# A two-block transformer kernel: the first stage's first block by lower and upper rows, an own place for odd heads' logits, and another order at the mixers' ends

## What is computed

```python
mod = (c_act @ w_ada[l] + b_ada[l]).reshape(B, N_MOD, D_MODEL)
h = modulate(rms_norm(x, norm_gain[l, 0]), mod[:, 0], mod[:, 1])
x = x + 0.5 * mod[:, 2][:, None, :] * swiglu(h, ffn_w_gate[l, 0], ffn_w_up[l, 0], ffn_w_down[l, 0])
h = modulate(rms_norm(x, norm_gain[l, 1]), mod[:, 3], mod[:, 4])
x = x + mod[:, 5][:, None, :] * hybrid_mixer(h, ...)
...
def swiglu(h, w_gate, w_up, w_down):
    return (jax.nn.silu(h @ w_gate) * (h @ w_up)) @ w_down
```

## Time and profile before

| | us |
|---|---|
| median of 3 runs (2724.70 to 2727.91) | 2726.28 |
| the profiled execution, its time | 2726.13 |
| its span | 2724.3 |
| PE busy with matmuls / DVE busy / ACT busy | 2656.0 / 1981.2 / 1299.1 |
| 1730 to 1800 (heads of a "b" mixer), 70 us: PE / DVE / ACT busy | 62.34 / 48.72 / 41.49 |
| a raw load from issue to landing: by source, medians | 4.9 to 7.2 |
| the slowest raw load on the chain that ended last (issued at 153.82) | 14.03 |

### The profile page before, as it was taken

The page is one execution under the profiler, slowest core; times in us unless marked ns, Lnnn a source line. Parts: engine busy times, 40 slices in busy tenths (PEclk is TensorE's granted clock), DMA queues, the critical chain, the costliest instruction groups (busy, mean ns, idle before and its releaser), DMA issues.

```text
span 2724.3 us, 34156 instructions
## 1 busy us (share of the span) xinstructions
PE 2656.0 (97%) x13951; PEld 2219.1 (81%) x13951; DVE 1981.2 (73%) x2243; ACT 1299.1 (48%) x1451; POOL 0.8 (0%) x6
## 2 busy tenths in 40 slices
PE   6999999999999999999999999899999999998998
PEld 3888877888888877788888899778888889987887
DVE  4767887877768878877877767677787786856754
ACT  2444565544434566544544534554454454445443
POOL 0000000000000000000000000000000000000000
PEclk8999999999999999999999999999999999999999
DMA  7876864677687864677777758437768767763752
GB/s 278 290 287 218 301 211 166 228 261 253 243 290 249 295 225 157 209 260 260 239 261 243 259 197 287 160 126 275 263 212 284 248 242 245 241 205 112 239 201 92
DMA packets 324595, 634.21 MB, mean 233 GB/s; under 512 B 12370, under 2 KB 92434, under 8 KB 324440
## 3 DMA queue, kind: packets, MB, share of 16 engines
q1 hardware_dynamic: 311904, 620.78, 66.4%
q10 hardware_dynamic: 12536, 11.25, 1.5%
HBM read 630.88 MB, written 8.97 MB: 235 GB/s over the span
## 4 chain that ended last, share of the span: by engine, by line
PE 86%; DVE 9%; ACT 2%; issue 1%; DMA 1%; ACTq 0%; DVEq 0%; SPq 0%
PE bank L1465 19%; PE bank L1467 19%; PE bank L1466 19%; PE acc L1465 8%; PE acc L1467 8%; PE acc L1466 7%; DVE w_both L970 3%; PE bank L1574 1%; PE bank L1526 1%; DVE softmax L1179 1%; PE bank L1719 1%; DVE x L1033 1%; PE acc L1702 1%; DVE w_extra L970 1%; DVE work L1031 1%
## 5 line engine op out<-in xcount | busy, mean ns | idle before, releaser
L970 DVE TENSOR_TENSOR w_both<-raw,w_both 128x2048 fp32r<-128x2048 f32 x412 | 941.4, 2289 | 492.2 <-ACT w_both L549 491.3
L549 ACT ACTIVATE w_both<-raw 128x2048 fp32r<-128x2048 f32 x412 | 786.2, 1912 | 525.5 <-PE bank L1467 326.1
L1465 PE MATMUL bank<-w_both,h 128*128 128x512 f32 (+1 forms) x2016 | 773.7, 384 | 2.1 <-DVE w_both L970 1.8
L1467 PE MATMUL bank<-w_both,h 128*128 128x512 f32 (+1 forms) x2016 | 759.3, 377 | 0.0
L1466 PE MATMUL bank<-w_both,h 128*128 128x512 f32 (+1 forms) x2016 | 758.5, 376 | 0.0
L1465 PEld LDWEIGHTS bank<-w_both,h 128*128 128x128 f32 x2016 | 380.3, 189 | 75.1 <-issue 4.4
L1467 PEld LDWEIGHTS bank<-w_both,h 128*128 128x128 f32 x2016 | 379.9, 188 | 70.8
L1466 PEld LDWEIGHTS bank<-w_both,h 128*128 128x128 f32 x2016 | 380.5, 189 | 66.4 <-issue 1.0
L1004 DVE SCALAR_TENSOR_TENSOR ada_sum<-raw,c_act,ada_sum 128x512 f32<-128x512 f32 x476 | 357.5, 751 | 14.1
L1465 PE MATMUL acc<-w_both,y 128*128 128x512 f32 x896 | 356.4, 398 | 0.9 <-DVE softmax L1179 0.9
L1467 PE MATMUL acc<-w_both,y 128*128 128x512 f32 x896 | 349.5, 390 | 0.0
(11 more groups left out here) (196 smaller groups left out, 2355.3 us busy)
## 6 DMA issues: line engine op xcount, KB each, us to landing
raw<-in_w_ada_all SPq DMA_DIRECT2D x136, 1024.0 KB, 5.3
raw<-in_w_in SPq DMA_DIRECT2D x128, 1024.0 KB, 5.6
raw<-in_ffn_gate_all SPq DMA_DIRECT2D x88, 1024.0 KB, 5.2
raw<-in_ffn_up_all SPq DMA_DIRECT2D x88, 1024.0 KB, 5.4
raw<-in_ffn_down_all SPq DMA_DIRECT2D x88, 1024.0 KB, 5.0
raw<-in_w_branch SPq DMA_DIRECT2D x12, 1024.0 KB, 7.2
raw<-in_w_out SPq DMA_DIRECT2D x8, 1024.0 KB, 5.1
raw<-in_w_conv_out SPq DMA_DIRECT2D x8, 1024.0 KB, 4.9
```

What stands on the lines that cost most here:

```text
L549: activate(halves_of[n][0], src, ACT.Copy).then_inc(high_ready.sem, 1)
L970: tensor(halves_of[n][1], raw_of("unit", s, k, 0)[0], halves_of[n][0].bitcast(F32), ALU.subtract).then_inc(low_ready.sem, 1)
L1465: mm(dst, a_h, b_h, start=start, stop=False, skip_group_check=True)
L1467: return mm(dst, a_l, b_h, start=False, stop=True, skip_group_check=True)
```

## The change

Six edits.

1. *Columns at the start.* The order of loads becomes: lower shift columns (0 to 511), lower scale columns (1024 to 1535), x, two units, then the upper shift and scale columns; each block in two loads of 1 MB. All four bias rows are multiplied first. Block 0 is summed by DVE, block 1 half by PE and half by DVE, block 2 by DVE, block 3 half and half. The sums lie in `acc` instead of the four banks.
2. *First block by rows.* In stage 0 units 1 and 2 change places, so that gate and up have first the units of the lower 512 rows. `first_block` does the lower rows of gate and up for both token tiles (48 matmuls), then the upper modulation, then the upper rows. Only then are the products formed.
3. *Odd heads.* In mixer "b" the logits of odd heads lie in `ada_sum` and `logits_odd` instead of `temp`; `logits(m)` waits for the turn of head m-2 instead of m-1 (in "a" it waited for that of m-2 before, too).
4. *Start of the heads.* The split of one unit moves behind the first normalized head (both mixers).
5. *Row parts between the heads* in "b": one half part now comes after the last turn.
6. *Ends of the mixers.* In "a" ACT copies the third output unit first; in both, DVE splits h, the unit, h in this order. `early` is gone: unit 0 is copied by ACT at the end, and split by DVE only after the first updates of x; unit 1 is copied and split after the first normalized rows.

```diff
+        logits_odd = nc.alloc_sbuf_tensor_at("logits_odd", [P, 768], F32, offset=y_at + (4 * 2 * S + 1152) * 4)
...
-            wide = {"a": P, "b": 3 * P}[kind]
-            first = 576 * (m % 2) if kind == "a" else 0
-            return temp[:, first:first + wide], temp[:, first + wide:first + 3 * wide]
+            if kind == "b":
+                return (ada_sum[:, 0:384], logits_odd[:, :]) if m % 2 else (temp[:, 0:384], temp[:, 384:1152])
+            first = 576 * (m % 2)
+            return temp[:, first:first + P], temp[:, first + P:first + 3 * P]
...
+                k = {1: 2, 2: 1}.get(k, k)
...
-            for p in range(3):
-                sp.dma_start(first_w[:, p], ada_cols[0][:, :, 512 * p:512 * p + 512]).then_inc(first_landed[p].sem, 16)
+            def first_load(q):
+                for part in range(2):
+                    c0 = FIRST_AT[q]
+                    sp.dma_start(first_w[:, q, 4 * part:4 * part + 4],
+                                 ada_cols[0][:, 4 * part:4 * part + 4, c0:c0 + 512]
+                                 ).then_inc(first_landed[q][part].sem, 16)
+
+            first_load(0)
+            first_load(1)
             sp.dma_start(x[:, :, :], t["x"].rearrange("b (t p) n -> p (b t) n", p=P)).then_inc(x_landed.sem, 16)
-            sp.dma_start(first_w[:, 3, 0:4], ada_cols[0][:, 0:4, 1536:2048]).then_inc(first_landed[3].sem, 16)
             load(0)
-            sp.dma_start(first_w[:, 3, 4:8], ada_cols[0][:, 4:8, 1536:2048]).then_inc(first_landed[4].sem, 16)
+            load(1)
+            first_load(2)
+            first_load(3)
             for m, (what, s, k, part) in enumerate(items):
-                if m:
+                if m >= 2:
...
             def end_of_mixer(s, first_out):
 
+                high(s, first_out + 2)
                 for half in range(2):
                     high_of_h(s, 0, half, 4)
-                high(s, first_out + 2)
                 high(s, first_out + 3)
                 for half in range(2):
                     high_of_h(s, 1, half, 4)
-                early(s)
+                high(s + 1, 0)
...
+                mixer = STAGES[s - 1] != "f"
                 update(s - 1, 0, 0)
                 update(s - 1, 0, 1)
+                if mixer:
+                    low(s, 0)
                 norm(s, 0)
                 first = 2 if s == 12 or STAGES[s] == "f" else 1
                 if s < 12:
+                    if mixer:
+                        low(s, 1)
...
-                    if m >= ago:
-                        dve.wait_ge(turned_done.sem, turned_done.at(s, TURNS[kind] * (m - ago + 1)))
+                    if m >= 2:
+                        dve.wait_ge(turned_done.sem, turned_done.at(s, TURNS[kind] * (m - 1)))
...
                 def begin_heads():
                     logits(0)
+                    if kind == "a":
+                        return
+                    normalize(0)
+                    low(s, gates_from + 3)
...
+                        if kind == "a" and i == 1:
+                            low(s, gates_from + 3)
...
+                        if kind == "b" and 0 < i < count:
...
-                for half in range(2):
-                    low_of_h(s, 0, half, 4)
+                low_of_h(s, 0, 0, 4)
+                low(s, WO_A + 2)
+                low_of_h(s, 0, 1, 4)
                 for half in range(2):
                     merge(s, 1, half, 2, WC + 1, 1, last=True)
-                low(s, WO_A + 2)
                 low(s, WO_A + 3)
                 for half in range(2):
                     low_of_h(s, 1, half, 4)
-                early(s)
...
+            first_sum(0, range(8))
+            first_sum(1, range(4, 8))
+            dve.wait_ge(zeros_ready.sem, 2)
+            dve.wait_ge(gain_landed.sem, 16)
+            for tt in range(TT):
+                spread(0, tt)
+            first_scale(0)
+            normed_half(0, 0, 0)
+            normed_half(0, 1, 0)
+            low(0, 0)
+            low_of_h(0, 0, 0)
             dve.wait_ge(table_landed.sem, 80)
...
+            low(0, 1)
+            low_of_h(0, 1, 0)
+            first_sum(2, range(8))
+            first_sum(3, range(4))
+            low(0, 2)
             first_scale(1)
             normed_half(0, 0, 1)
-            low(0, 1)
             low_of_h(0, 0, 1)
-            normed_half(0, 1, 0)
             normed_half(0, 1, 1)
-            low(0, 2)
             low(0, 3)
+            low_of_h(0, 1, 1)
...
+                def first_block():
+
+                    gate(0, 0, 0)
+                    turn_h(s, 1, 0)
+                    up(0, 0, 0)
+                    gate(0, 1, 0)
+                    pe.wait_ge(table_ready.sem, 2)
+                    up(0, 1, 0)
+                    first_summed(2, 20)
+                    first_direct(3, range(4, 8))
+                    first_summed(3, 24)
+                    turn_h(s, 0, 1)
+                    gate(0, 0, 1)
+                    turn_h(s, 1, 1)
+                    up(0, 0, 1)
+                    gate(0, 1, 1)
+                    turn_hidden(0, 0)
+                    up(0, 1, 1)
...
                         if kind == "b" and 1 <= i <= count:
                             turn(i - 1)
+                        if kind == "b" and i == count:
+                            between(i + 1)
...
                 def between(i):
-                    pe.wait_ge(logits_ready.sem, logits_ready.at(s, 16))
-                    pe.wait_ge(y_ready.sem, y_ready.at(s, 2))
-                    rows(0, 0)
-                    rows(0, 1, (0,))
+                    if i == HEADS["b"]:
+                        pe.wait_ge(logits_ready.sem, logits_ready.at(s, 16))
+                        pe.wait_ge(y_ready.sem, y_ready.at(s, 2))
+                        rows(0, 0)
+                    else:
+                        rows(0, 1, (0,))
...
+            for q in range(4):
+                mm(first_acc(q), ones[0:1, :], first_bias[q], start=True, stop=False, skip_group_check=True)
+            first_direct(1, range(4))
+            first_summed(0, 8)
+            first_summed(1, 12)
...
```

211 lines of the change are left out of this document (108 added, 103 removed).

## The result

The changed kernel takes **2691.0 us** (median of 4 runs, 2689.7 to 2691.9) against 2726.5 of before in the same session: a ratio of 0.987, 95% interval 0.9853 to 0.9887, so 35.4 us less, where 27.8 were forecast. The profiled execution has a span of 2689.3 us against 2724.3, 35.0 less, so the trace can be asked where they come from.

What follows compares the result with a forecast made beforehand. PE bounds the kernel, busy 2656 of 2724.3 us, its waits ended mostly by DVE. Terms 0.7 + 2.1 + 14.5 + 10.5 = 27.8 us off 2726.1 give 2698.3 us; range 2690.5 to 2713.9.

Steps and rivals of the forecast that it cites:

- C: Rival, first stage: the clock rises while the one-row bias matmuls run, giving 2695.5 us; chance 0.08.
- First stage: Start of the kernel: PE's first unit starts 18.8 us sooner, but DVE then sets the pace, leaving 0.7 us gain.
- I count 18.8: First stage: DVE's work and small waits from the first "up" product to the split PE needs, 19.6 us before.
- Heads "a": Start of mixer "a"'s heads: PE's 1.05 us wait for the first normalized head goes, twice, 2.1 us.
- Heads "b": Mixer "b"'s heads: earlier first head and logits not waiting for the turn give 6.7 and 7.8 us, together 14.5.
- 1.4 and 1.0: Mixer "b"'s heads: gains in us counted for the two pairs of heads in a pass.
- Ends: Ends of the four mixers: reordered splits and updates remove PE waits, 1.4 us remaining at the other tile's turn; 10.5 us.
- A: Rival: the first stage costs instead of giving, PE's pieces running at half clock behind waits; 2703.8 us at -4.8; chance 0.17.
- B: Rival, mixer "b"'s heads: ACT takes over as the limit, gain only 9.4 us, 2703.4 us; chance 0.11.
- D: Rival, mixers' ends: the wait only moves to the next tile's turn, and B as well; 2708.4 us; chance 0.08.
- E: Rival, mixers' ends: loads into slots freed later come too late and each next stage stands; slower, 2731.6 us; chance 0.02.
- The table load: First stage: ACT's load before the first silu takes 1.28 us by its row; by the skill page, 1.2 us longer.

Runs made afterwards that it cites:

- e1: Changed kernel with the first stage's part undone (loads, bias rows, first block as before): 2694.4 us.
- e6: Changed kernel, PE turning the other tile's lower half before the first twelve matmuls in the first stage, not behind them: 2690.0 us.
- e9: Changed kernel with only the place of the third output unit's split at the mixers' ends put back: 2694.9 us.
- e2: Changed kernel with the whole order at the mixers' ends put back as before: 2702.8 us.
- e7: Changed kernel, DVE in the first stage forming the second product before unit 5's split and splitting the second tile's y before the four sums: 2691.7 us.
- e10: e7 with 32 raw loads cut to a quarter, an eighth or a half of their 1 MB: 2687.1 us, against 2689.7 for the changed kernel so cut.
- e3: Kernel before with only the own place for odd heads' logits in mixer "b" added: 2719.4 us.
- e5: Changed kernel with DVE's split of the fourth gate unit in mixer "b"'s heads moved behind the third normalized head: 2688.2 us.
- e8: Changed kernel with three edits together: late split in "b" heads, early turn and DVE's other order in the first stage: 2689.9 us.

## Why the prediction was right

The time (2698.3 forecast, 2691.0 measured) lies in the range, the sign is right, and the mechanisms of all four terms came as described; every term was too small, by 7.6 us in all. The time is only 0.5 us above the low end, which was made of the clock's rise (C) and 5 us more in the heads. Neither came: that the range still holds the sum of four small misses is partly luck.

- **First stage, 0.7 forecast, 3.2 between the two traces, 3.8 by e1, 4.1 as the mean of traces.** The mechanism was right: half a block early, then DVE's pace, with two waits of PE (3.8 forecast, 3.2 measured). The size was off in two steps. "The first up product can start at 67.5": it started at 65.84. The four bias rows took 7.1 us and not 8.1, but the eight direct matmuls behind them 6.6 and not 5.9, so the first unit's matmul was only 0.2 sooner than forecast. Most of the rest is the 48 matmuls: "PE ends its 48 matmuls at 48.5" gives them 14.9 us from 33.6, while the forecast's own prices (5.1 for twelve at half clock, 0.5 for the transposes, 0.23 for each of the other 36) make 13.9, and they took 13.6 (33.38 to 47.02). The upper columns' new scale came at 52.7 and not at 54.0. "I count 18.8" for DVE's chain: 18.2. These 1.7 and 0.6 us are 2.3 of the 2.5 that were missing. The sentence that the sums come "only then", behind the other tile's split, described what happens but not what limits: with that split 3.7 us sooner (e6) the product gained 0.9.
- **Heads "a", 2.1 forecast, 2.6 measured** (1.2 + 1.3). PE's wait of 1.05 at the first turn is gone in both. Read from the two traces alone; it had no experiment, so the cause is argued.
- **Heads "b", 14.5 forecast, 17.0 measured.** The first piece was right: 3.1 forecast, and the third part of the second head's turn went from 1738.29 to 1723.77, 14.5 less 11.4 that were there before, so 3.2. The new wait was to be 1.6 and is 1.57. The pairs were mis-sized: "1.4 and 1.0", measured 1.8 and 1.5. I had compared DVE's 6.7 us for an odd head with PE's 6.2 as if each head had to come out even; over the pair DVE has less work than PE (12.3 against 13.2 us), so its lead from the even head carries it through the odd one. The last piece was 1.4 for 1.2, and the second pass gave 1.2 more than the first for its clock, 1.1 forecast.
- **Ends, 10.5 forecast, 12.8 measured.** The wait at the other tile's turn was mis-sized. "It then reaches the other tile's turn at 21.4 and waits 1.4 there": on the same count PE arrives at 22.05, 0.28 of it by the new wait on the unit's split, and the rows come at 22.5 instead of 22.8, so it waits 0.49. The rows of before could have said so for the arrival: there PE arrived at 24.15, and without the waits of 1.56 and 0.71 that is 21.9. In the sum, DVE's way from the last split of h to those rows became 2.0 us shorter at the first end and 1.8 at each of the other three, against 1.6 and 1.4 forecast, which is 1.3 of the 2.3 us that were missing; the other 1.0 lies ahead of that split, where the pieces are 1.1 and 1.2 us in "a" and 1.6 twice in "b", against 0.88 and 1.4. As waits, 0.88 and 1.32 come back when the unit's place is undone (e9).
- **What was not in the sum**: -0.5 in a stage that the change doesn't touch, where PE waits 0.32 at 796.73, behind a split of y that follows on a unit's landing, and did not before; 0.2 is not placed.
- **The rivals.** A is refuted by e1. B: ACT ends waits in the heads, but of 0.17 to 0.25 each. C: PE's pace did not rise while the one-row matmuls ran (below), and half clock in the start is as long as before. D: the wait does not move, e9 and e2. E as put (loads into slots freed later at the mixers' ends) did not come; no wait of PE there is on a load. Its kin exists elsewhere: loads are what the early start runs up against (e7, e10).
- **The table load.** In the changed first stage the scalar engine's table load of 1.28 us lies ahead of the first silu, as forecast, and the silu follows at its end (timeline of ACT):

```profile
63.63 1.28 ACT L652 ACT_TABLE_LOAD   x1
64.93 0.60 ACT L652 ACTIVATE temp<-bank 128x512 f32<-128x512 f32 x1
```

By the 2.66 us of the Trainium skill, "ScalarE: Activation LUTs", section "What ACT_TABLE_LOAD costs", the product would have come about 1.1 us later, as an estimate (63.63 + 2.66, and 0.60 for the silu, is 66.9 against 65.84). The trace does not agree in this place: 1.30 from the load's start to the activation's.

What stays open: why one feed-forward stage's load comes in time in one run and 1.5 to 3 us late in the next (e3, e5, e8), and whether the changed kernel's slack there is the same in all its runs. In both places, near 171 and near 800, the late unit is the one that SP issues next behind a copy of the bias tables (`table_store`), and there DMA moves little: 101 GB/s from 150 to 154 in the changed kernel, where it moves 356 from 140 to 150. The kernel before had its slowest load of the chain there too (issued at 153.82, 14.03 us). Whether that copy makes the unit late no run here tests.

## What to carry to other kernels

Put a value on each wait with what stands right behind it: a wait that ends by an engine's own order, with idle time before the next one, was worth its full length (the ends, the late split), and one whose removal brings the engine to a load that is not there was worth nothing or less (DVE's order in the first stage). Ask too whether the load comes sooner with the gain: what was gained ahead of the first product took it along, what was gained behind it did not. For a change of many parts, take one instruction behind each part in both traces and compare starts: it gives every part its share, and it shows at once when a share belongs to no part. Where two engines alternate with unequal steps, compare their work over the whole period, not step by step.
